# Meta keys of a head pair taken together in block 1's attention, and three convolution rows made ready one unit earlier

## The chip, the cores and the metric

The kernel runs on one core of a Trainium2 chip. The metric is the device time of one execution in microseconds (us). The names of the engines are those of the profile: PE multiplies matrices (PEld is its loading of weights), DVE works on vectors, ACT applies functions and copies, POOL is the general engine, SP issues the transfers.

## The reference, cut to what matters

The program is two transformer blocks on 256 tokens of width 1024. The change lies in the first one, whose mixer joins attention and a short convolution. The attention has 8 heads, each token sees 16 learned meta tokens and all tokens up to itself:

```python
N_META = 16; BLOCK = 128; N_HEADS = 8; QK_NOPE, QK_ROPE, V_DIM = 64, 32, 64
# for a block of 128 queries that starts at s0, keys = meta tokens + tokens:
s = (jnp.einsum('bqhd,bkhd->bhqk', qn_b, k_nope)
     + jnp.einsum('bqhr,bkr->bhqk', qr_b, k_rope)) * ATTN_SCALE
mask = (k_idx[None, :] >= PAD_FRONT) & (k_idx[None, :] <= q_idx[:, None])
p = jax.nn.softmax(jnp.where(mask[None, None], s, NEG_INF), axis=-1)
attn_block = jnp.einsum('bhqk,bkhd->bqhd', p, v)

u = gate_c * x_in                                    # the convolution beside it
y = sum(conv_w[k] * u_pad[:, k:k + plen] for k in range(CONV_W))
conv = gate_b * y
merged = concat([rms_norm(attn, attn_out_norm), rms_norm(conv, conv_out_norm)])
return merged @ w_out
```

Behind it come a routed mixture of 32 experts with a shared one, and the second block (pooling, windowed attention, a gated feed-forward part). They are not touched.

## The kernel before

The kernel is written out engine by engine: each engine has its own list of instructions, in the order of the code, and waits on counters (`s["..."]`) that other engines raise. No scheduler moves anything. An engine that waits holds up all that stands behind it in its list.

Block 1's attention is a loop over 16 **units** `u`. A unit is one head and one tile of 128 queries: `head_and_tile(u)` gives head 2·(u//4) + u%2 and tile u%4//2, so four units are a pair of heads with both tiles. Tile 0 sees 144 keys (16 meta, 128 tokens), tile 1 sees 272. Per unit:

- PE: `scores(u + 2)`, a share of other work, at every fourth unit `values` of the pair before, then `turn_probs(u)`, which turns the probabilities so that keys lie on the partitions (2 turns of 128 x 128 for tile 0, 3 for tile 1, the last one nearly empty: 16 keys).
- DVE: masked maximum of unit u (L1244), reciprocal and scaling of unit u-1 (L1250, L1251), then `beside(u)`.
- ACT: exponential of unit u (L739), two copies of the turned probabilities of unit u-1 from PSUM to SBUF (L748 for the full tiles, L749 for the 16 rows left over), then `beside(u)`.

The share of other work on PE is first the convolution: `conv_part(6)` to `conv_part(11)` in units 0 to 5, each 24 multiplications (three products of high and low halves, eight times), then from unit 7 on (`FILL = 7`) the convolution's rows times their part of `w_out`: `conv_share(j, m)`, two of them per unit, each 3 multiplications of 512 columns. `conv_share` with row tile m waits for `convg_done` m+1, and for the split weights.

For that, `beside` on ACT and DVE carries the convolution along. For each of the four row tiles m: ACT copies a gate out of PSUM (`conv_gate`, L670, which also frees the PSUM bank into which a later `conv_part` writes); DVE multiplies and adds the taps (`conv_taps`, L1160 to L1169) and the second gate (`conv_gated`, L1173); ACT squares the row tile (`conv_square`, L674) and makes its scaled high half (L725, counter `mrg_high`); DVE makes the low half (L1229, counter `convg_done`). Between these, ACT and DVE split weights into high and low halves of 1024 columns (`split_high_half` L403, `split_low_half` L410).

Before the change ACT makes the four high halves in unit 7 and DVE the four low ones in unit 8; `conv_gate(3)` stands in unit 5 behind a weight split. On PE `conv_part(11)` of unit 5 waits for `gc_sb` 4, which is `conv_gate(3)`.

`values(m, i)` multiplies the turned probabilities of a pair by its values: 4 multiplications for tile 0, 6 for tile 1, each of 64 columns of values with 128 queries; the two heads stand in the two halves of the PE columns and run side by side. The last pair's call stands behind the last unit, ahead of `mix_share`, the attention's rows times their part of `w_out`.

All weights come in 1 MB pieces through one SP queue, in the order of use. A piece is issued when PE (`split_used`, `used`) or another counter says that its place is free. Around the change these are: two work pieces that wait for `conv_done` and `convg_done` (L581), two ring pieces that wait for `split_used` of unit 15 (L592), three pieces that wait for the last `o_ps` (L581).

## Time and profile before

| | us |
|---|---|
| median of 3 runs | 682.7 (682.45 to 682.95) |
| the profiled execution | 681.71 |
| its span in the profile | 679.9 |

| engine | busy us, share of the span |
|---|---|
| PE | 629.5 (93%) |
| DVE | 356.8 (52%) |
| ACT | 293.8 (43%) |
| POOL | 49.3 (7%) |

The profile is of one execution. Times in its rows count from the start of the span. A timeline row gives start, duration, engine, source line, what is written and read, and how often; in square brackets stands the idle time of the engine ahead of it and what ended that. A row with xN is N instructions in a run, its duration from the first start to the last end. An fp32 multiplication on PE shows as two records, a turn of 128 columns as one. PEclk is the granted TensorE clock: 1.00 is 2.4 GHz, 0.50 is 1.2 GHz.

### The profile page before, as it was taken

The numbers are of one execution on the slowest core, as the hardware profiler recorded it, in microseconds if no ns is written. First come the engines' busy times: TensorE is split into PE (matmuls) and PEld (weight loads), VectorE is DVE, ScalarE is ACT, GpSimd is POOL, SyncE is SP. The second block draws the span as 40 slices with busy tenths as digits, with TensorE's granted clock in tenths as the row PEclk, the third lists the DMA queues.
The fourth block names the chain that finished last, engine by engine and source line by source line (L and its number), as shares of the span: only waits on it lengthen the run. The fifth ranks groups of instructions, "written<-read, shape, count | busy, mean of one in ns | idle before, by whom it ended". The sixth has DMA issues, their size and how long they took to land.

```text
span 679.9 us, 10209 instructions
## 1 busy us (share of the span) xinstructions
PE 629.5 (93%) x4027; PEld 471.7 (69%) x4027; DVE 356.8 (52%) x689; ACT 293.8 (43%) x560; POOL 49.3 (7%) x74
## 2 busy tenths in 40 slices
PE   8999799999999766779899999999999999999996
PEld 5979677842543321334389999898788888888884
DVE  5687664831130120110088886757856666666665
ACT  6855562421111010100085765554655555555554
POOL 2100101100010000000048100000000000000001
PEclk9999999999999976979999999999999999999999
DMA  8966328989999999999997443355535555555101
GB/s 345 421 231 240 126 123 330 408 362 425 428 388 421 421 421 419 423 421 421 421 422 291 155 150 124 124 187 187 185 134 192 196 199 193 195 193 185 63 1 62
DMA packets 26286, 180.73 MB, mean 266 GB/s; under 512 B 3184, under 2 KB 3312, under 8 KB 5120
## 3 DMA queue, kind: packets, MB, share of 16 engines
q1 hardware_dynamic: 25200, 177.60, 66.1%
q10 hardware_dynamic: 1040, 2.50, 0.9%
q8 instruction: 32, 0.52, 0.3%
q14 instruction: 14, 0.11, 0.1%
HBM read 179.04 MB, written 1.05 MB: 265 GB/s over the span
## 4 chain that ended last, share of the span: by engine, by line
PE 69%; DMA 15%; DVE 8%; ACT 5%; issue 2%; POOLq 0%; SPq 0%; POOL 0%; ACTq 0%; DVEq 0%
PE ps L1614 66%; DMA ring<-stream_dram 15%; PE ps L1617 3%; DVE ring_r L410 2%; ACT single L403 1%; DVE work L1549 1%; ACT work L889 1%; DVE work L1552 1%; DVE h L1602 0%; DVE work L1605 0%; ACT turned L894 0%; ACT work_r L885 0%; DVE extra_r L509 0%; DVE work L1430 0%; ACT work L799 0%
## 5 line engine op out<-in xcount | busy, mean ns | idle before, releaser
L1614 PE MATMUL ps<-turned,single 128*128 128x256 f32 (+2 forms) x944 | 231.3, 326 | 2.6 <-ACT work L670 1.8
L1614 PE MATMUL ps<-turned,ring_r 128*128 128x256 f32 (+1 forms) x648 | 179.8, 281 | 0.0
L1614 PEld LDWEIGHTS ps<-turned,single 128*128 128x128 f32 x944 | 156.3, 189 | 19.5 <-ACT work L670 2.4
L410 DVE TENSOR_TENSOR ring_r<-ring,single 128x1024 fp32r<-128x1024 f32 (+1 forms) x132 | 160.3, 1237 | 13.6 <-ACT single L403 13.4
L403 ACT ACTIVATE single<-ring 128x1024 fp32r<-128x1024 f32 (+1 forms) x132 | 134.1, 1047 | 0.1
L1614 PEld LDWEIGHTS ps<-turned,ring_r 128*128 128x128 f32 x648 | 121.1, 188 | 0.4
L1614 PE MATMUL ps<-ring,work 128*32 128x512 f32 (+2 forms) x462 | 71.0, 621 | 16.6 <-DMA ring<-stream_dram 14.3
L1614 PE MATMUL ps<-single,turned 128*128 128x512 f32 (+3 forms) x208 | 60.2, 369 | 2.9 <-DVE turned L1229 2.2
L1614 PEld LDWEIGHTS ps<-single 128*128 128x128 f32 x257 | 38.3, 188 | 34.2 <-issue 20.8
L1614 PE MATMUL ps<-single 128*128 128x512 f32 (+1 forms) x257 | 55.2, 353 | 3.4 <-DVE single L1441 2.3
L1614 PE MATMUL ps<-single,work_r 128*128 128x512 f32 x176 | 56.2, 392 | 0.0
L1614 PEld LDWEIGHTS ps<-ring,work 128*32 128x32 f32 (+1 forms) x462 | 19.9, 120 | 49.8 <-issue 23.2
L1582 DVE TENSOR_TENSOR work<-work,ps 128x512 f32<-128x512 f32 x22 | 15.1, 688 | 60.0 <-ACT work L919 59.8
L919 ACT ACTIVATE work<-ps 128x512 f32<-128x512 f32 x22 | 13.2, 598 | 73.1 <-PE ps L1614 73.1
L1614 PEld LDWEIGHTS ps<-single,turned 128*128 128x128 f32 (+1 forms) x208 | 36.7, 183 | 10.5 <-issue 2.5
L806 ACT ACTIVATE work<-ps 128x256 f32<-128x256 f32 x8 | 3.1, 384 | 91.6 <-PE ps L1614 91.6
L1614 PE MATMUL ps<-work 128*64 128x128 f32 (+7 forms) x272 | 38.8, 373 | 2.6 <-DVE work L1087 1.8
L1430 DVE TENSOR_TENSOR work<-work,ps 128x256 f32<-128x256 f32 x8 | 3.4, 422 | 70.4 <-ACT work L806 70.4
L1441 DVE SCALAR_TENSOR_TENSOR single<-ps,work,single 128x512 fp32r<-128x512 f32 x16 | 12.0, 751 | 52.7 <-ACT single L812 52.7
L1614 PEld LDWEIGHTS ps<-single,work_r 128*128 128x128 f32 x176 | 33.0, 187 | 7.3
L1614 PE MATMUL ps<-ring,turned_w 128*32 128x512 f32 x208 | 30.1, 688 | 8.0 <-DMA ring<-stream_dram 5.8
L1614 PE MATMUL ps<-ring_r,turned 128*128 128x512 f32 (+3 forms) x104 | 36.9, 363 | 0.0
(260 smaller groups left out, 703.6 us busy)
## 6 DMA issues: line engine op xcount, KB each, us to landing
ring<-stream_dram SPq DMA_DIRECT2D x145, 1024.0 KB, 11.9
work<-stream_dram SPq DMA_DIRECT2D x12, 1024.0 KB, 12.3
turned_w<-stream_dram SPq DMA_DIRECT2D x4, 1024.0 KB, 14.0
extra<-stream_dram SPq DMA_DIRECT2D x2, 1024.0 KB, 11.6
ring<-stream_dram SPq DMA_DIRECT2D x2, 832.0 KB, 7.6
h<-x_dram SPq DMA_DIRECT2D x2, 512.0 KB, 4.6
gain<-gains_dram ACTq DMA_DIRECT2D x2, 512.0 KB, 10.4
yields<-stream_dram SPq DMA_DIRECT2D x1, 1024.0 KB, 12.3
```

Source lines behind the costliest of these rows:

```text
L403: act.activation(w_hi[k % HIGHS][:, a], ring[:, place, a], ACT.Copy).then_inc(s["whi_done"], 1)
L410: dve.tensor_tensor(ring_r[:, place, a], ring[:, place, a], w_hi[k % HIGHS][:, a].bitcast(F32), ALU.subtract).then_inc(s["wlo_done"], 1)
L806: act.activation(sg, ps[:, 4, 0:FF], ACT.Silu).then_inc(s["sg_done"], 1)
L889: act.activation(gate[:, m, :], gate[:, m, :], ACT.Sigmoid).then_inc(s["sig_done"], 1)
L919: act.activation(fpart[:, m % 2, :].rearrange("p (a b) -> p a b", b=TOK), ffn_banks(m)[:, :, TOK:2 * TOK], ACT.Copy).then_inc(s["fsg_done" ...
L1430: dve.tensor_tensor(htok, sg, ps[:, 4, FF:2 * FF], ALU.mult).then_inc(s["ht_done"], 1)
L1441: dve.scalar_tensor_tensor(yl[:, n * 512:(n + 1) * 512], ps[:, 6 + n, :], wsl[:, p:p + 1], yh[:, n * 512:(n + 1) * 512].bitcast(F32), ALU. ...
L1549: dve.tensor_tensor(gate[:, m, :], gate[:, m, :], ps[:, 2 + m % 4, :], ALU.mult).then_inc(s["br_sb"], 1)
L1552: dve.tensor_tensor(gate[:, m, 0:TOK], gate[:, m, 0:TOK], gate[:, m, TOK:2 * TOK], ALU.add).then_inc(s["mg_sum"], 1)
L1582: dve.tensor_tensor(halves(fsum[:, m % 2, :], TOK), halves(fpart[:, m % 2, :], TOK), ffn_banks(m)[:, :, 0:TOK], ALU.add).then_inc(s["fh_su ...
L1614: return pe.matmul(o, lhsT, rhs, start=start, stop=stop, **kw)
L1617: return pe.transpose(o, a, ident[0:rows, 0:rows])
```

## The change

Each unit's 16 meta probabilities are scaled into a tile of their own, `pm1_meta`, where the two heads of a pair lie 32 columns apart in 64 columns with zeros between. They are turned once for both heads, at the odd unit, and multiplied with `v1_meta`, whose rows for the other head are zero. The tokens' keys now fill whole tiles of 128, and a multiplication of `values` takes both query tiles at once. ACT's `conv_gate(3)` goes from unit 5 to unit 4, ahead of the weight split; three of the high halves go to unit 6, the fourth stays at unit 7, and a weight split goes from unit 6 to unit 7; DVE's low halves go to units 7 and 8, and its `conv_taps(3)` ahead of a weight split.

```diff
             for i in range(NT):
                 act.wait_ge(s["v_ps"], i + 1)
+                act.activation(v1[i], ps[:, 4 + i, :], ACT.Copy).then_inc(s["v_sb"], 1)
+            act.wait_ge(s["v_ps"], NT + 1)
+            for j in range(2):
+                last = act.activation(v1_meta[j * META * 2:j * META * 2 + META, :].rearrange("p (a b) -> p a b", b=2 * VD)[:, :, j * VD:(j + 1) * VD],
+                                      ps[0:META, 6, :].rearrange("p (a b) -> p a b", b=2 * VD)[:, :, j * VD:(j + 1) * VD], ACT.Copy)
...
+                if u == 4:
+                    conv_gate(3)
                 if 2 <= u < 6:
                     split_high_half(act, 8 + (u - 2) // 2, u % 2)
                 if u == 5:
-                    conv_gate(3)
                     conv_square(2)
                 if u == 6:
+                    act.wait_ge(s["conv_ps"], 3 * CT)
+                    for m in range(CT - 1):
+                        conv_high(m)
+                if u == 7:
+                    conv_square(3)
+                    conv_high(CT - 1)
                     split_high_half(act, 10, 0)
-                if u == 7:
-                    act.wait_ge(s["conv_ps"], 3 * CT)
-                    conv_square(3)
-                    for m in range(CT):
-                        act.activation(mrg_hi[:, CT + m, :], mrg[:, m, :], ACT.Copy, ...
...
-                    act.activation(pt1[i][:, w % 2, 0:full_k], ps[:, 3 + w % 2, 0:full_k], ACT.Copy)
-                    act.activation(pt1[i][0:META, w % 2, full_k:full_k + P], ps[0:META, 3 + w % 2, full_k:full_k + P],
-                                   ACT.Copy).then_inc(s["pt_sb"], 1)
+                    i, j = w % 4 // 2, w % 2
+                    last = act.activation(pt1[:, j, i * P:(2 * i + 1) * P], ps[:, 3 + j, 0:(1 + i) * P], ACT.Copy)
+                    if j:
+                        last = act.activation(pt1_meta[0:4 * META, i * P:(i + 1) * P], ps[0:4 * META, 3 + j, TOK:TOK + P], ACT.Copy)
+                    last.then_inc(s["pt_sb"], 1)
...
                 if u == 6:
+                    conv_taps(3)
                     split_low_half(dve, 9, 1)
-                    conv_taps(3)
                 if u == 7:
                     conv_gated(3)
+                    conv_low(0)
+                    conv_low(1)
                 if u == 8:
-                    for m in range(CT): ...
+                    conv_low(2)
+                    conv_low(3)
...
-                    dve.tensor_scalar(pm1[:, w % 3, 0:nk], pm1[:, w % 3, 0:nk], rinv[:, w:w + 1], None, ALU.mult
+                    dve.tensor_scalar(pm1_meta[:, w % 4 // 2, w % 2 * 2 * META:w % 2 * 2 * META + META], pm1[:, w % 3, 0:META],
+                                      rinv[:, w:w + 1], None, ALU.mult)
+                    dve.tensor_scalar(pm1[:, w % 3, META:nk], pm1[:, w % 3, META:nk], rinv[:, w:w + 1], None, ALU.mult
...
-                for k in range(2 + head_and_tile(u)[1]):
-                    last = turn(ps[:, 3 + u % 2, k * P:(k + 1) * P], pm1[:, u % 3, k * P:(k + 1) * P])
+                i, j = u % 4 // 2, u % 2
+                for k in range(1 + i):
+                    last = turn(ps[:, 3 + j, k * P:(k + 1) * P], pm1[:, u % 3, META + k * P:META + (k + 1) * P])
...
+                if j:
+                    last = turn(ps[0:4 * META, 3 + j, TOK:TOK + P], pm1_meta[:, i, :])
...
-                u = 4 * m + 2 * i
-                pe.wait_ge(s["pt_sb"], u + 2)
+                pe.wait_ge(s["pt_sb"], 4 * (m + 1))
...
-                for k in range(2 + i):
+                for n, (v, a, lo) in enumerate(((v1[0], 0, 0), (v1[1], 2 * P, P), (v1_meta, None, 0))):
                     for j in range(2):
                         c = (2 * m + j) * VD
-                        last = mm(ps[j * VD:(j + 1) * VD, 6 + m % 2, i * P:(i + 1) * P], v1[k][:, c:c + VD],
-                                  pt1[i][:, j, k * P:(k + 1) * P], i == k == 0, i == 1 and k == 1 + i, skip_group_check=True)
+                        last = mm(ps[j * VD:(j + 1) * VD, 6 + m % 2, lo:TOK], v[:, c:c + VD],
+                                  pt1_meta if a is None else pt1[:, j, a:a + TOK - lo], n == 0, n == 2, skip_group_check=True)
```

Three places in the lists of instructions show what moved. First ACT, from unit 4 to unit 7, before the change. L403 is a weight split, L670 `conv_gate`, L674 `conv_square`, L725 the high halves, L748 and L749 the copies of turned probabilities.

```order
L749 ACTIVATE work<-ps 16x128
L403 ACTIVATE single<-ring 128x1024 [waits slot_full3,split_used]
L739 ACTIVATE work,stat<-work,stat 128x144 [waits nm_done]
L748 ACTIVATE work<-ps 128x128 [waits pt_ps]
L749 ACTIVATE work<-ps 16x128
L403 ACTIVATE single<-ring 128x1024
L670 ACTIVATE work<-ps 128x258 [waits cu_done,conv_ps]
L674 ACTIVATE work<-work 128x256 [waits conv_done]
L739 ACTIVATE work,stat<-work,stat 128x272 [waits nm_done]
L748 ACTIVATE work<-ps 128x128 [waits pt_ps]
L749 ACTIVATE work<-ps 16x128
L403 ACTIVATE single<-ring 128x1024 [waits slot_full4,split_used]
```

The same place on ACT with the change; L671 is `conv_gate` there, L404 a weight split, L675 `conv_square`, L678 a high half, L758 and L760 the copies.

```order
L760 ACTIVATE work<-ps 64x128
L671 ACTIVATE work<-ps 128x258 [waits cu_done,conv_ps]
L404 ACTIVATE single<-ring 128x1024 [waits slot_full3,split_used]
L750 ACTIVATE work,stat<-work,stat 128x144 [waits nm_done]
L758 ACTIVATE work<-ps 128x128 [waits pt_ps]
L404 ACTIVATE single<-ring 128x1024
L675 ACTIVATE work<-work 128x256 [waits conv_done]
L750 ACTIVATE work,stat<-work,stat 128x272 [waits nm_done]
L758 ACTIVATE work<-ps 128x128 [waits pt_ps]
L760 ACTIVATE work<-ps 64x128
L678 ACTIVATE turned<-work,vec 128x256 [waits conv_ps]
L678 ACTIVATE turned<-work,vec 128x256 x2
```

The gate copy has passed two weight splits and an exponential, the weight split of unit 6 has made way for three high halves, and the even unit has one copy of probabilities instead of two.

Second DVE, units 6 and 7, before the change: L1251 is the scaling of probabilities, L410 a weight split, L1160 to L1169 `conv_taps(3)`, L1244 the masked maximum (with a second instruction that reads it out).

```order
L1251 TENSOR_SCALAR work<-work,stat 128x144 [waits dve_step]
L410 TENSOR_TENSOR ring_r<-ring,single 128x1024 [waits whi_done]
L1160 TENSOR_TENSOR work<-work,ps 128x258 [waits conv_ps,gc_sb]
L1165 TENSOR_TENSOR work<-work 128x258 [waits z_sb,cu_done]
L1167 TENSOR_SCALAR work<-work,vec 128x256 [waits dve_step]
L1168 SCALAR_TENSOR_TENSOR work<-work,vec 128x256 [waits dve_step]
L1169 SCALAR_TENSOR_TENSOR work<-work,vec 128x256 [waits dve_step]
L1244 ISA work,stat<-ps,cst 128x272 [waits s_ps,dve_step]
```

The same place with the change; L1260 and L1262 are the two scalings, L411 the weight split.

```order
L1260 TENSOR_SCALAR work<-work,stat 128x16 [waits dve_step]
L1262 TENSOR_SCALAR work<-work,stat 128x128
L1165 TENSOR_TENSOR work<-work,ps 128x258 [waits conv_ps,gc_sb]
L1170 TENSOR_TENSOR work<-work 128x258 [waits z_sb,cu_done]
L1172 TENSOR_SCALAR work<-work,vec 128x256 [waits dve_step]
L1173 SCALAR_TENSOR_TENSOR work<-work,vec 128x256 [waits dve_step]
L1174 SCALAR_TENSOR_TENSOR work<-work,vec 128x256 [waits dve_step]
L411 TENSOR_TENSOR ring_r<-ring,single 128x1024 [waits whi_done,dve_step]
L1253 ISA work,stat<-ps,cst 128x272 [waits s_ps]
```

The taps stand ahead of the split, and each unit has one scaling more, of 16 columns.

Third PE, the last unit and the last `values`, before the change: L1617 is a turn, the rows with `ps<-work 64x128` are `values`, the last row is the first of `mix_share`.

```order
L1617 MATMUL ps<-cst,work 128x128 [waits pt_sb,p_done]
L1617 MATMUL ps<-cst,work 128x128 x2
L1614 MATMUL ps<-work 64x128 [waits att_low,pt_sb]
L1614 MATMUL ps<-work 64x128 x3
L1614 MATMUL ps<-work 64x128 [waits pt_sb]
L1614 MATMUL ps<-work 64x128 x5
L1614 MATMUL ps<-single,turned 128x512 [waits att_low,wlo_done,cm_sb]
```

The same place with the change.

```order
L1628 MATMUL ps<-cst,work 128x128 [waits pt_sb,p_done]
L1628 MATMUL ps<-cst,work 128x128
L1628 MATMUL ps<-cst,work 64x128
L1625 MATMUL ps<-work 64x256 [waits att_low,pt_sb]
L1625 MATMUL ps<-work 64x256
L1625 MATMUL ps<-work 64x128 x2
L1625 MATMUL ps<-work 64x256 x2
L1625 MATMUL ps<-single,turned 128x512 [waits att_low,wlo_done,cm_sb]
```

Two waits for copied probabilities, with four multiplications between them, have become one wait ahead of all six; the third turn writes 64 rows instead of 128.

## Rows read from the trace of the kernel before

**Rows 1.** The chain that ended last, in order: start us, us, what.

```profile
75.83 0.27 ACT work L670
...
82.58 0.67 DVE turned L1229
83.38 2.77 PE ps L1614 x6
...
205.46 13.52 DMA ring<-stream_dram
```

**Rows 2.** Stretches: us; busy of PE, PEld, DVE, ACT, POOL; PEclk; DMA share; GB/s.

```profile
90.00:100.00 10.00, 9.87 (x66) 7.78 (x65) 7.98 (x21) 6.96 (x22) 0.74 (x1) 1.00 0.01 2
...
190.00:200.00 10.00, 9.48 (x77) 4.07 (x79) 4.87 (x13) 2.14 (x4) 2.39 (x3) 1.00 0.96 378
...
210.00:220.00 10.00, 9.38 (x47) 3.21 (x45) 0.75 (x1) 1.07 (x2) 0.00 (x0) 1.00 1.01 424
```

**Rows 3.** Timeline of SP: the first transfers behind the last units.

```profile
104.14 0.80 SPq L592 DMA_DIRECT2D ring<-stream_dram  x2
106.58 1.30 SPq L581 DMA_DIRECT2D work<-stream_dram  x3
```

**Rows 4.** Timeline of units 5 and 6, PE and ACT.

```profile
75.73 0.36 ACT L670 ACTIVATE work<-ps 128x258 f32<-128x258 f32 x1
...
76.15 0.51 PE L1614 MATMUL ps<-turned,single 128*128 128x256 f32 x2 [1.26 <-ACT work L670]
...
79.13 0.38 PE L1617 MATMUL ps<-cst,work 128*128 128x128 f32 x2
79.34 0.41 PE L1614 MATMUL ps<-work 128*128 128x144 f32 x2
...
79.87 1.04 ACT L403 ACTIVATE single<-ring 128x1024 fp32r<-128x1024 f32 x1
...
80.41 0.55 PE L1617 MATMUL ps<-cst,work 128*128 128x128 f32 x3 [0.66 <-DVE work L1251]
```

**Rows 5.** Timeline of unit 7: the high and low halves, and PE behind them.

```profile
82.05 1.69 ACT L725 ACTIVATE turned<-work,vec 128x256 fp32r<-128x256 f32 x4
...
82.58 1.84 DVE L1229 SCALAR_TENSOR_TENSOR turned<-work,vec,turned 128x256 fp32r<-128x256 f32 x4 [0.56 <-ACT turned L725]
83.38 0.64 PE L1614 MATMUL ps<-single,turned 128*128 128x512 f32 x1 [2.17 <-DVE turned L1229]
...
86.58 0.80 PE L1614 MATMUL ps<-work 128*128 128x272 f32 x2
```

**Rows 6.** Stretches of 1 us in both waits; columns as in rows 2.

```profile
75.00:76.00 1.00, 0.00 (x0) 0.00 (x0) 0.14 (x1) 1.00 (x2) 0.00 (x0) 1.00 0.00 0
...
84.00:85.00 1.00, 1.00 (x4) 0.81 (x3) 0.96 (x6) 0.14 (x2) 0.00 (x0) 0.50 1.02 426
```

**Rows 7.** Timeline of PE: a weight load behind `values`, and unit 8.

```profile
73.98 0.20 PEld L1617 LDWEIGHTS ps<-cst,work 128*128 128x128 f32 x2 [0.17 <-issue]
...
88.14 0.40 PE L1614 MATMUL ps<-ring_r,turned 128*128 128x512 f32 x1
88.38 0.40 PE L1614 MATMUL ps<-single,turned 128*128 128x512 f32 x1
88.70 1.31 PE L1614 MATMUL ps<-work 128*64 128x128 f32 x20
```

**Rows 8.** Timeline of the attention's end, PE and ACT.

```profile
104.50 0.55 PE L1617 MATMUL ps<-cst,work 128*128 128x128 f32 x3 [0.17 <-DVE work L1251]
104.98 1.56 PE L1614 MATMUL ps<-work 128*64 128x128 f32 x20
...
105.37 0.25 ACT L749 ACTIVATE work<-ps 16x128 f32<-16x128 f32 x1
106.47 0.50 PE L1614 MATMUL ps<-single,turned 128*128 128x512 f32 x1
```

**Rows 9.** Groups of DVE by form: busy us, mean ns, idle before.

```profile
L1436 DVE TENSOR_SCALAR work<-work 128x16 f32<-128x16 f32 x1 | 0.2, 175 | 0.0
```

More of the change, by code:

```diff
@@ L674, in conv_square, with conv_high @@
                 act.activation(sq[:, CT + m, :], mrg[:, m, :], ACT.Square).then_inc(s["sq_done"], 1)
+            def conv_high(m):
+                act.activation(mrg_hi[:, CT + m, :], mrg[:, m, :], ACT.Copy,
+                               scale=vec[:, V_GCONV + m:V_GCONV + m + 1]).then_inc(s["mrg_high"], 1)
             split_high(act, 4)
@@ L697, in _ @@
             act.wait_ge(s["pad_done"], 1)
-            for i, m in enumerate((P, P, META)):
+            for i in range(NT):
                 act.wait_ge(s["v_ps"], i + 1)
-                act.activation(v1[i][0:m, :], ps[0:m, 4 + i, :], ACT.Copy).then_inc(s["v_sb"], 1)
+                act.activation(v1[i], ps[:, 4 + i, :], ACT.Copy).then_inc(s["v_sb"], 1)
[3 more added lines that the diff above has]
+                                      ps[0:META, 6, :].rearrange("p (a b) -> p a b", b=2 * VD)[:, :, j * VD:(j + 1) * VD], ACT.Copy)
+            last.then_inc(s["v_sb"], 1)
             for hp in range(0, HEADS // 2, 2):
@@ L1174, in conv_gated, with conv_low @@
                                   ).then_inc(s["conv_done"], 1)
+            def conv_low(m):
+                dve.wait_ge(s["mrg_high"], m + 1)
+                dve.scalar_tensor_tensor(mrg_lo[:, CT + m, :], mrg[:, m, :], vec[:, V_GCONV + m:V_GCONV + m + 1],
+                                         mrg_hi[:, CT + m, :].bitcast(F32), ALU.mult, ALU.subtract).then_inc(s["convg_done"], 1)
             conv_taps(0)
@@ L1840, in _ @@
                 if u and u % 4 == 0:
-                    values(u // 4 - 1, 0)
-                    values(u // 4 - 1, 1)
+                    values(u // 4 - 1)
                 turn_probs(u)
@@ L1857, in mix_share @@
                         last.then_inc(s["mix_ps"], 1)
-            values(CT - 1, 0)
-            values(CT - 1, 1)
+            values(CT - 1)
             pe.wait_ge(s["cm_sb"], 2 * NT)
```

46 lines of the change are left out of this document (16 added, 30 removed).

## The prediction

> **What bounds the kernel now.** I read the chain of waits first, then the stretches, then the timeline of the stage that changes. In the chain the reader is to see three things [rows 1]: it passes through ACT's gate copy (L670) at 75.83 us and through the low halves of the convolution (L1229) at 82.58 us, runs on PE behind them, and from 205.46 us on it waits for weight transfers. So a gain in the attention must also reach the transfers to count. The stretches answer that [rows 2]: from 90 to 100 us the queue moves 2 GB/s, it is empty, since places for weights are not free yet; its next pieces are issued at 104.14 and 106.58 us, released by PE in the last unit and by the last `values` [rows 3]. From 210 on it moves 424 GB/s at a share of 1.01. Between, at 190 to 200 us, its share is still 0.96: it waits for PE there. The stream therefore begins when the attention ends and its last gap is closed by PE. If the attention ends X earlier, both PE and the stream move by X, and the end too.
>
> In the timeline of the attention PE is busy except for two places. In unit 5 it stands 1.26 us for the gate copy, which ACT makes at 75.73 only because a weight split is ahead of it [rows 4]. In units 6 and 7 it waits 0.66 us for the scaling of unit 6 [rows 4] and 2.17 us for the first low half [rows 5]. Behind this second wait the granted clock is 0.50, which is 1.2 GHz; in the first wait, and behind it, it stayed at 1.00 [rows 6].
>
> **The change part by part.** Gains have a plus.
>
> *Gate copy in unit 4.* `conv_gate(3)` needs `conv_part(9)`, done a unit before, so it no longer ends last. What is late next for `conv_part(11)` is PE itself. +1.26 [rows 4].
>
> *High and low halves in units 6 to 8.* Before, the first `conv_share` begins at 83.38, that is 1.33 after ACT begins the high halves at 82.05 [rows 5]. With the change the high halves stand where the weight split stood that began at 79.87 [rows 4], right behind the copy of unit 5. On the old times the first share begins at 79.87 + 1.33 = 81.20, which is 2.18 earlier. PE would be ready at about 80.2 (scores at 79.34, three turns and one more scores behind), so some 1.0 us of waiting is left. The wait of 0.66 for the scaling is inside these 2.18: the taps pass the weight split on DVE and the gate comes earlier, so the maxima of units 7 and 8 no longer queue behind both. +2.18. Bounds: the rest of the wait goes wholly (+3.2), or one more weight split of 1.04 stays ahead (+1.1).
>
> *The clock.* From 83.38 to 86.58, 3.20 us, PE runs at 0.50 [rows 5, 6]. If the remaining wait of 1.0 does not lower the clock, and the 1.26 did not, the same work takes half of it. +1.6. Bounds: 0 and +1.6.
>
> *Turns.* A pair has 2 + 2 + 3 + 3 turns before and 1 + 2 + 2 + 3 now, 8 fewer in four pairs. Two turns take from 79.13 to 79.34, 0.11 each [rows 4]. +0.9; where PE waits beside one it is worth nothing, so 0 to +0.9.
>
> *Columns of PE changed over.* The eight turns of meta keys have 64 columns, between turns and scores of 128. The rows show what such a change costs at `values`: the last two multiplications of a share stand 0.24 apart, the first of `values` 0.32 behind the last (88.14, 88.38, 88.70), 0.08 more, and behind `values` no weights are loaded for 0.17 us [rows 7]. Each of the eight goes in and out, but the last one is followed by `values`, in the same mode: 15 changes. I take 0.10, nearer to the difference of starts, since an idle weight load is partly covered: -1.5, with 1.2 and 2.6 as ends. The Trainium skill (TensorEngine Tiling (Array Packing), Key Properties) says that changing the tiling mode drains the engine; the trace agrees with its 0.08, the page has no price.
>
> *`values`.* 10 multiplications of 128 queries become 4 of 256 and 2 of 128: the same 640 columns streamed for each head, so no gain. But the last one now waits for the whole copy. Before, its first four multiplications ran from 104.98 beside the copies, the rest followed at the copy's end, 105.37 + 0.25 = 105.62, and `mix_share` began at 106.47 [rows 8]. Now all 1.31 us [rows 7] stand behind 105.62, which gives 106.93: -0.5. For the first three pairs a share or a `conv_part` lies between copy and `values` and hides it.
>
> *DVE and ACT.* Each unit has one scaling of 16 columns more; the only such row takes 0.175 us [rows 9]. It counts where PE waits for the scaling, as at 104.50 [rows 8]; about one unit in each pair after the first, so -0.2, with 0 and 16 x 0.175 = -2.8 as ends. ACT drops one of two copies (0.25 us) in the eight even units; PE covers that, so 0. The longer clearing on POOL and the two copies of meta values lie before the loop, beside `conv_part(4)` and `(5)`: 0; uncovered, the second copy would cost about the 0.25 of such a copy.
>
> *Transfers.* The two work pieces that wait for `conv_done` and `convg_done` are issued some 2 to 4 us earlier, into an empty queue. 0.
>
> Sum: 1.26 + 2.18 + 1.6 + 0.9 - 1.5 - 0.5 - 0.2 = 3.7 us. Against the profiled execution, 681.71, that is 678.0. This execution was 1.0 below the median of 682.7, so for the median I predict 682.7 - 3.7 = 679.0.
>
> **The rivals.** Two runs of this kernel apart by less than 0.2%, 1.4 us, are not told apart.
>
> *The narrow turn takes two passes.* A turn shows as one record, an ordinary fp32 multiplication as two: `values` has 20 records for 10 [rows 7]. If the 64-column turn is run like an ordinary one, each of the eight costs 0.11 more, 0.9 in all: 679.9. Against it: no turn of 64 columns is in the trace; that the turned data pass through exactly needs no second pass. The Trainium skill (same page, Gotcha 2) says that column tiling excludes the transpose mode for fp32 input; by that rule this case would be the likely one, and no row here can show it.
>
> *The wait for the low halves stays long.* If ACT reaches the high halves late (its instruction waits for the end of all convolution parts, behind the copy of unit 5) the wait is again near 2 us, and the clock falls again: 1.6 and about 1.1 of the 2.18 are lost, 682.7 - 1.0 = 681.7. For it: the clock did fall behind 0.66 + 2.17. Against it: the copy ahead of it is released by a turn that PE makes right after the last part.
>
> *The stream takes it.* If transfers and not PE set the time of the stage behind, nothing is left: 682.7. For it: the chain is on transfers from 205 us [rows 1]. Against it: the queue moves 2 GB/s at 90 to 100 us and is restarted by PE [rows 2, 3].
>
> *Slower.* The mode changes drain more than `values` shows, because a turn is only 0.11 long and the scores and shares behind it queue up. Without their price the sum is 5.2; the 15 changes decide from 0.35 us each (5.2 / 15), and at 0.44 the kernel is slower by 1.4: 684.1. Against it: 0.08 to 0.17 at `values` [rows 7].
>
> *Changes for nothing.* If a turn of 64 columns is loaded like any other, the 1.5 fall away: 677.5.
>
> **How the numbers follow.** Forecast 0.60, two passes 0.12, wait stays 0.08, stream 0.06, slower 0.05, changes for nothing 0.09. Forecast's own range: 1.1 less by the mode changes' upper end and 0.9 less by turns beside waits give 681.0; 0.3 more by their lower end, and the rest of the wait gone (1.0), 677.7. The range for all reaches a little past the free changes and to the long wait: 677.2 to 681.6. Faster: 0.60 + 0.12 + 0.09 = 0.81; within the bound: 0.14; slower: 0.05.
>
> **What would show it.** Right: no PE wait for the gate copy in unit 5; the first share of 512 columns about 3.4 us (1.26 + 2.18) earlier; no stretch at 0.50 between 75 and 100 us; a step of about 0.1 us on either side of each 64-column turn; a wait of some 0.6 us ahead of the last `values`; the transfer of 106.58 at about 102.9, and the first transfer wait of 205.46 about 3.7 earlier. Wrong: two records for a turn of meta keys; a clock of 0.50 behind the first share; the first transfers earlier but the wait at 205 unmoved; or a new wait for scalings in most units.

## The result and the profile after

| | before | after |
|---|---|---|
| median of 8 runs | 682.95 (682.1 to 684.41) | 678.44 (676.41 to 679.84) |
| ratio of the times, 95% interval | | 0.9928 (0.9914 to 0.9941) |
| profiled execution, its span | 681.71, 679.9 | 676.90, 675.1 |

The change makes the kernel 0.7% faster, 4.9 us by the ratio. The forecast was 679.0 with a range of 677.2 to 681.6. Profiled execution against profiled execution the sum of the forecast's terms was 3.7 us and the measured difference is 4.8: the direction and the main mechanism were right, and one term stood for a cost that is not there.

The timeline of PE of the changed kernel, from the first `values` to the first row of `mix_share`, answers to the PE rows of [rows 4, 5, 7, 8]. L1625 is a multiplication, L1628 a turn.

```profile
72.73 1.30 PE L1625 MATMUL ps<-work 128*64 128x256 f32 x12
...
74.39 0.60 PE L1625 MATMUL ps<-turned,single 128*128 128x256 f32 x2
...
77.44 0.38 PE L1628 MATMUL ps<-cst,work 128*128 128x128 f32 x2
77.66 0.41 PE L1625 MATMUL ps<-work 128*128 128x144 f32 x2
...
79.35 0.47 PE L1625 MATMUL ps<-single,turned 128*128 128x512 f32 x1 [0.75 <-DVE turned L1183]
...
81.41 0.59 PE L1625 MATMUL ps<-single,turned 128*128 128x512 f32 x1
...
90.62 0.55 PE L1628 MATMUL ps<-cst,work 128*128 128x128 f32 x3 [0.39 <-DVE work L1262]
...
98.96 0.55 PE L1628 MATMUL ps<-cst,work 128*128 128x128 f32 x3 [0.41 <-DVE work L1262]
100.14 1.30 PE L1625 MATMUL ps<-work 128*64 128x256 f32 x12 [0.63 <-ACT work L760]
101.37 0.50 PE L1625 MATMUL ps<-single,turned 128*128 128x512 f32 x1
```

Two rows of the kernel before belong beside them, its first `values` and unit 8's share:

```profile
72.74 1.31 PE L1614 MATMUL ps<-work 128*64 128x128 f32 x20
...
87.01 0.60 PE L1614 MATMUL ps<-single,turned 128*128 128x512 f32 x1
```

The row at 74.39 is `conv_part(11)`: no wait in brackets is left, where it stood at 76.15 with 1.26. The first share stands at 79.35 instead of 83.38, 4.03 earlier; its wait is 0.75 instead of 2.17 us. From it to unit 8's share (81.41, before 87.01) it is 2.06 instead of 3.63 us. The last row, `mix_share`, is 5.10 earlier than at 106.47 [rows 8]. Three rows show what the change gives back: the waits for scalings at 90.62 and 98.96, and 0.63 us ahead of the last `values`, which stood without a wait before.

The halves and the clock: ACT makes the high halves (L678) and DVE the low ones (L1183) in the changed kernel:

```profile
78.19 1.29 ACT L678 ACTIVATE turned<-work,vec 128x256 fp32r<-128x256 f32 x3
...
78.72 0.88 DVE L1183 SCALAR_TENSOR_TENSOR turned<-work,vec,turned 128x256 fp32r<-128x256 f32 x2 [0.53 <-ACT turned L678]
```

Stretches of the changed kernel, in the columns of [rows 2]:

```profile
79.00:80.00 1.00, 0.65 (x3) 0.60 (x4) 0.82 (x4) 1.00 (x5) 0.00 (x0) 1.00 0.80 164
90.00:100.00 10.00, 8.71 (x50) 6.26 (x49) 6.63 (x24) 6.47 (x22) 0.73 (x1) 1.00 0.09 16
100.00:110.00 10.00, 9.86 (x53) 7.88 (x54) 2.73 (x7) 0.83 (x3) 1.01 (x1) 1.00 0.99 417
190.00:200.00 10.00, 10.00 (x84) 3.85 (x76) 2.52 (x4) 1.37 (x2) 2.39 (x3) 1.00 0.94 362
...
210.00:220.00 10.00, 8.38 (x56) 4.06 (x55) 1.68 (x3) 1.76 (x3) 0.00 (x0) 1.00 1.01 423
```

The granted clock is 1.00 behind the wait of 0.75, so the stretch at 0.50 of [rows 6] is gone. The share of the transfers still has a gap at 190 to 200 and is full at 210, as in [rows 2]. SP's issues and the first long transfer in the chain:

```profile
98.36 0.80 SPq L593 DMA_DIRECT2D ring<-stream_dram  x2
101.48 1.29 SPq L582 DMA_DIRECT2D work<-stream_dram  x3
```

```profile
195.23 8.31 DMA ring<-stream_dram
```

The issue of 106.58 [rows 3] stands at 101.48, 5.10 earlier, as much as `mix_share`; 4.8 of it reach the end of the span. The wait of 195.23 has no counterpart in the chain of before. The next long one has; first before, then after, it starts 5.04 and ends 4.25 earlier:

```profile
220.70 18.16 DMA ring<-stream_dram
```

```profile
215.66 18.95 DMA ring<-stream_dram
```

### The profile page after: what moved, and what is told of

Its sections match the earlier page's. It is cut to its first block, busy times and chain, and to the rows that moved or that the text cites. A ratio compares the mean times of both kernels' runs of the same rounds, so it can differ in the third digit from the quotient of the medians.

```text
span 675.1 us, 10135 instructions
## 1 busy us (share of the span) xinstructions
PE 628.7 (93%) x3987; PEld 470.5 (70%) x3987; DVE 359.2 (53%) x705; ACT 292.9 (43%) x553; POOL 49.4 (7%) x72
## 3 DMA queue, kind: packets, MB, share of 16 engines
HBM read 179.04 MB, written 1.05 MB: 267 GB/s over the span
## 4 chain that ended last, share of the span: by engine, by line
PE 71%; DMA 14%; DVE 8%; ACT 4%; issue 2%; POOLq 0%; SPq 0%; POOL 0%; ACTq 0%; DVEq 0%
PE ps L1625 68%; DMA ring<-stream_dram 14%; PE ps L1628 3%; DVE ring_r L411 2%; ACT single L404 1%; DVE work L1560 1%; ACT work L900 1%; DVE work L1563 1%; DVE h L1613 0%; DVE work L1616 0%; ACT turned L905 0%; ACT work_r L896 0%; DVE extra_r L510 0%; DVE work L1441 0%; ACT work L810 0%
## 5 line engine op out<-in xcount | busy, mean ns | idle before, releaser
L1625 PE MATMUL ps<-turned,single 128*128 128x256 f32 (+2 forms) x944 | 231.5, 327 | 1.3 <-DVE turned L1578 0.6
L1625 PE MATMUL ps<-turned,ring_r 128*128 128x256 f32 (+1 forms) x648 | 179.7, 281 | 0.0
L1625 PEld LDWEIGHTS ps<-turned,single 128*128 128x128 f32 x944 | 156.4, 189 | 18.0 <-issue 2.0
L411 DVE TENSOR_TENSOR ring_r<-ring,single 128x1024 fp32r<-128x1024 f32 (+1 forms) x132 | 159.8, 1233 | 11.2 <-ACT single L404 11.0
L404 ACT ACTIVATE single<-ring 128x1024 fp32r<-128x1024 f32 (+1 forms) x132 | 134.1, 1047 | 0.1
L1625 PEld LDWEIGHTS ps<-turned,ring_r 128*128 128x128 f32 x648 | 121.1, 188 | 0.4
L1625 PE MATMUL ps<-ring,work 128*32 128x512 f32 (+2 forms) x462 | 71.0, 621 | 18.1 <-DMA ring<-stream_dram 15.8
L1625 PEld LDWEIGHTS ps<-single 128*128 128x128 f32 x257 | 38.3, 189 | 33.9 <-issue 20.5
L1625 PE MATMUL ps<-single,turned 128*128 128x512 f32 (+3 forms) x208 | 59.2, 364 | 1.6 <-DVE ring_r L411 0.9
L1625 PE MATMUL ps<-single 128*128 128x512 f32 (+1 forms) x257 | 55.3, 353 | 3.5 <-DVE single L1452 2.3
L1625 PE MATMUL ps<-single,work_r 128*128 128x512 f32 x176 | 56.2, 392 | 0.0
L1625 PEld LDWEIGHTS ps<-ring,work 128*32 128x32 f32 (+1 forms) x462 | 19.9, 120 | 50.4 <-issue 24.8
L1625 PEld LDWEIGHTS ps<-single,turned 128*128 128x128 f32 (+1 forms) x208 | 36.2, 181 | 9.0 <-DVE ring_r L411 1.6
L1625 PE MATMUL ps<-work 128*64 128x128 f32 (+7 forms) x240 | 38.5, 400 | 3.2 <-DVE work L1092 1.8
L1625 PEld LDWEIGHTS ps<-single,work_r 128*128 128x128 f32 x176 | 33.0, 187 | 7.3
L1028 POOL TENSOR_SCALAR stat<-stat 128x1 f32<-128x1 f32 (+1 forms) x7 | 4.7, 666 | 437.5 <-ACT ps L945 177.7
L1625 PE MATMUL ps<-ring_r,turned 128*128 128x512 f32 (+3 forms) x104 | 36.4, 358 | 0.0
```

The costliest lines, as they stand in the source:

```text
L404: act.activation(w_hi[k % HIGHS][:, a], ring[:, place, a], ACT.Copy).then_inc(s["whi_done"], 1)
L411: dve.tensor_tensor(ring_r[:, place, a], ring[:, place, a], w_hi[k % HIGHS][:, a].bitcast(F32), ALU.subtract).then_inc(s["wlo_done"], 1)
L1028: pool.tensor_scalar(ms, ss, 1.0 / D, EPS, ALU.mult, ALU.add).then_inc(s["pool_step"], 1)
L1625: return pe.matmul(o, lhsT, rhs, start=start, stop=stop, **kw)
```

## The experiments

All kernels are compared inside one stage, since executions of one kernel differ by 2 to 3.5 us (682.10 to 684.41 before, 676.41 to 679.84 after), as much as many of the effects. The **count** is the time from the start of the first `values` to the start of the first row of `mix_share`. "To share" is from the first `values` to the first share of 512 columns, "to unit 8" from there to unit 8's share. Us, from the timelines of PE, one profiled execution per kernel; the ratio is that of the times to the kernel before, with its interval. The first `values` start between 72.58 and 74.68 us in these executions, so points in time that the expectations name, such as `mix_share` at 101.1, shift by up to 2 us; the differences do not.

| kernel | to share | to unit 8 | count | ratio |
|---|---|---|---|---|
| before | 10.64 | 3.63 | 33.73 | |
| after | 6.62 | 2.06 | 28.64 | 0.9928 (0.9914 to 0.9941) |
| e1_rows | 6.75 | 2.07 | 28.28 | 0.9923 (0.9904 to 0.9943) |
| e2_meta | 10.20 | 3.60 | 33.74 | 0.9988 (0.9976 to 1.0000) |
| e3_gate | 10.33 | 3.64 | 33.45 | 1.0001 (0.9990 to 1.0013) |
| e4_warm | 10.64 | 2.05 | 32.17 | 0.9963 (0.9949 to 0.9977) |
| e8_taps | 9.11 | 3.86 | 33.37 | 0.9972 (0.9955 to 0.9989) |
| e9_high | 8.49 | 2.05 | 30.01 | 0.9943 (0.9921 to 0.9966) |
| e5_wide | 6.63 | 2.06 | 28.61 | 0.9925 (0.9904 to 0.9947) |
| e6_tail | 6.62 | 2.46 | 28.68 | 0.9915 (0.9893 to 0.9937) |
| e7_early | 6.08 | 2.77 | 28.47 | 0.9922 (0.9900 to 0.9945) |
| e10_order | 6.08 | 2.78 | 28.18 | 0.9932 (0.9910 to 0.9955) |
| e11_rows_early | 6.23 | 2.24 | 27.94 | 0.9939 (0.9918 to 0.9959) |
| e12_low | 6.08 | 2.36 | 27.88 | 0.9925 (0.9908 to 0.9941) |

The first question is which half of the change gains, the rows or the meta keys. **The rows alone** (e1_rows):

```diff
+                if u == 4:
+                    conv_gate(3)
                 if 2 <= u < 6:
...
                 if u == 5:
-                    conv_gate(3)
...
                 if u == 6:
+                    act.wait_ge(s["conv_ps"], 3 * CT)
+                    for m in range(CT - 1):
+                        conv_high(m)
+                if u == 7:
+                    conv_square(3)
+                    conv_high(CT - 1)
                     split_high_half(act, 10, 0)
...
                 if u == 6:
+                    conv_taps(3)
                     split_low_half(dve, 9, 1)
-                    conv_taps(3)
                 if u == 7:
                     conv_gated(3)
+                    conv_low(0)
+                    conv_low(1)
...
```

> The kernel before with the changed order of the convolution rows alone (gate copy in unit 4, three high halves in unit 6, the fourth in unit 7, low halves in units 7 and 8, taps ahead of the split); the meta keys are turned and multiplied as before. Theory (the rows are the gain, the meta keys nearly nothing): conv_part(11) at 74.4 to 74.6 instead of 76.15, the first share of 512 columns at 79.5 to 80.1 instead of 83.38, granted clock 1.00 throughout 75 to 100 us, mix_share at 101.1 to 101.7 instead of 106.47, the time 4.8 to 5.4 us under the kernel before. The forecast's own terms give 1.26 + 2.18 + 1.6 = 5.0 here as well. Rival (much of the gain came from the meta keys, that is from fewer turns and multiplications): gain of 3 us or less, mix_share at 103 or later.

```profile
73.33 1.31 PE L1623 MATMUL ps<-work 128*64 128x128 f32 x20
...
80.08 0.47 PE L1623 MATMUL ps<-single,turned 128*128 128x512 f32 x1 [0.66 <-DVE turned L1183]
...
101.61 0.50 PE L1623 MATMUL ps<-single,turned 128*128 128x512 f32 x1
```

The count is 28.28, a gain of 5.45, and the clock stays at 1.00: the whole gain and 0.36 more than the full change has in this count. **The meta keys alone** (e2_meta) is the changed kernel with these places put back:

```diff
-                if u == 4:
-                    conv_gate(3)
...
-                    conv_low(0)
-                    conv_low(1)
...
```

> The changed kernel with the order of the convolution rows put back as before; the meta keys of a pair are still turned and multiplied together. Theory (a turn of 64 columns between turns of 128 is free; eight turns fewer give 0.9 at most, the scalings of 16 columns and the last values take 0.5 to 1.0): both waits of 1.3 and 2.2 us and the stretch at clock 0.50 are back, mix_share between 106.2 and 106.8 (before: 106.47), the time within 0.5 us of the kernel before. The forecast's terms (0.9 - 1.5 - 0.5 - 0.2): 1.3 us slower, mix_share at 107.8.

```profile
76.45 0.51 PE L1621 MATMUL ps<-turned,single 128*128 128x256 f32 x2 [1.13 <-ACT work L671]
...
83.50 0.77 PE L1621 MATMUL ps<-single,turned 128*128 128x512 f32 x1 [1.98 <-DVE turned L1181]
```

The waits are back, and the stretch at 0.50 with them. The count is that of before, 33.74 for 33.73. Only ahead of it does the meta part show a gain: from the first turn to the first `values` 14.69 us (58.61 to 73.30) instead of 14.90 (57.84 to 72.74). So the forecast's 1.3 us of loss for the meta part is not there. The time's ratio leaves anything from no change to 1.6 us.

Of this, **the price of the column change** was tried by itself (e5_wide), a meta turn of full width in the changed kernel:

```diff
-                    last = turn(ps[0:4 * META, 3 + j, TOK:TOK + P], pm1_meta[:, i, :])
+                    last = turn(ps[:, 3 + j, TOK:TOK + P], pm1_meta[:, i, :])
```

> The changed kernel with the meta turn 128 columns wide instead of 64 (the 64 further columns hold zeros and their result is not read), so that no change of column width stands between turns and scores. Theory (a change of width costs nothing here): step of 0.11 us for this turn as for the others, from the first values to mix_share 28.5 to 28.8 us as in the changed kernel (28.64), time within 0.2 us of it. The forecast's term (15 changes of 0.10): 1.4 us less for the whole attention, 27.6 in this count (three quarters of the turns lie in it). Rival by 0.17 a change: 2.5 us less.

The count is 28.61 for 28.64. PE's timeline has the same two turns of unit 5 here, both 128 wide:

```profile
79.19 0.38 PE L1628 MATMUL ps<-cst,work 128*128 128x128 f32 x2
79.41 0.41 PE L1625 MATMUL ps<-work 128*128 128x144 f32 x2
```

They take 0.22 us up to the scores. In the changed kernel, where the second of them has 64 columns, it is 0.22 as well (77.44 to 77.66), and in the kernel before 0.21 [rows 4]. The groups by form of the changed kernel show the narrow turns with no time idle ahead of them (the last column):

```profile
L1628 PE MATMUL ps<-cst,work 128*64 128x128 f32 x8 | 2.2, 272 | 0.0
```

A change of width costs nothing here, and eight records for eight turns refute the rival of two passes. The Trainium skill (TensorEngine Tiling (Array Packing), Key Properties) has a change of the tiling mode drain the engine; this trace shows no such time at a turn of 64 columns.

Next the parts of the rows. **The gate copy alone** (e3_gate):

```diff
+                if u == 4:
+                    conv_gate(3)
                 if u == 5:
-                    conv_gate(3)
```

> The kernel before with one edit: the gate copy conv_gate(3) in unit 4 instead of unit 5. Theory: conv_part(11) at 74.4 to 74.6 instead of 76.15, that is 1.6 to 1.8 earlier; ACT still makes the high halves behind the weight split of unit 6, so the first share of 512 columns moves less than that, to between 82.0 and 83.0, the wait ahead of it grows to 2.5 to 3.5 us, and the granted clock falls to 0.50 behind it as before; gain in time 0.4 to 1.4 us. Rival (the two waits are one chain, and the gate alone takes both away): first share before 81.5, clock 1.00, gain 3 us or more.

The wait of 1.26 is gone, the count is only 0.28 lower, and the time has not changed. PE's timeline in units 6 and 7 shows where it went:

```profile
80.26 0.55 PE L1618 MATMUL ps<-cst,work 128*128 128x128 f32 x3 [2.20 <-DVE work L1252]
82.91 0.54 PE L1615 MATMUL ps<-single,turned 128*128 128x512 f32 x1 [1.86 <-DVE turned L1230]
```

Before, the waits were 1.26 + 0.66 + 2.17 = 4.09 us; now they are 2.20 + 1.86 = 4.06. The expectation that the last of them grows was wrong, and with it the gain of 0.4 to 1.4 us: the time went to the wait before it. DVE's timeline names the holder:

```profile
75.71 1.23 DVE L410 TENSOR_TENSOR ring_r<-ring,single 128x1024 fp32r<-128x1024 f32 x1 [2.59 <-ACT single L403]
...
76.85 0.42 DVE L1161 TENSOR_TENSOR work<-work,ps 128x258 f32<-128x258 f32 x1
...
79.28 0.44 DVE L1245 CUSTOM_DVE_ANT_0 work<-ps,cst 128x272 f32<-128x272 f32 x1
```

DVE waits 2.59 us for ACT's weight split, makes its own, and only then the taps (from 76.85) and the maximum that the scaling needs. **Gate and taps** (e8_taps) take that away:

```diff
+                if u == 4:
+                    conv_gate(3)
...
                 if u == 5:
-                    conv_gate(3)
...
                 if u == 6:
+                    conv_taps(3)
                     split_low_half(dve, 9, 1)
-                    conv_taps(3)
```

> The gate copy in unit 4 (which alone moved the wait of 1.26 us to the scaling of unit 6, 2.20 us) together with conv_taps(3) ahead of the weight split on DVE in unit 6; the high and low halves stay in units 7 and 8. Counted from the start of the first values to the start of mix_share (before 33.73, gate alone 33.45, all row edits 28.28). Theory (the taps behind the split held the scaling, so gate and taps are one step): no wait for the scaling of unit 6 above 0.3 us; the high halves still stand behind a weight split and unit 7's work on ACT, so the first share comes 1.0 to 1.9 us earlier than before in this count and waits 2 to 3 us, the clock falls to 0.50 behind it; 31.9 to 32.8, gain in time 0.9 to 1.8 us. Rival (gate and taps do nothing without the high halves): 33.2 to 33.7. Rival (they do it all): 28.3 to 29.5, clock 1.00.

The wait for the scaling is gone and the first share comes 1.53 us earlier in this count, as the theory had it; but the count gains 0.36 in all, as the first rival had it. PE's timeline, and stretches in the columns of [rows 2], the last one from the kernel before:

```profile
82.50 0.77 PE L1615 MATMUL ps<-single,turned 128*128 128x512 f32 x1 [3.00 <-DVE turned L1230]
```

```profile
82.00:83.00 1.00, 0.50 (x1) 0.50 (x2) 1.00 (x3) 1.00 (x4) 0.07 (x1) 0.50 1.03 434
...
87.00:88.00 1.00, 1.00 (x3) 0.74 (x3) 0.74 (x2) 1.00 (x2) 0.00 (x0) 0.50 0.99 393
88.00:89.00 1.00, 1.00 (x6) 0.54 (x4) 0.46 (x4) 0.57 (x3) 0.00 (x0) 0.81 0.30 123
```

```profile
86.00:87.00 1.00, 1.00 (x6) 0.93 (x5) 0.00 (x0) 0.17 (x1) 0.00 (x0) 0.54 1.08 459
```

All the waiting stands in one place now, 3.00 us, and the clock is at 0.50 until past 88, where before it rose at 86.9. Of the 1.53 us that the first share gained, 0.23 are lost up to unit 8's share and 0.94 behind it (20.40 us from there to `mix_share`, before 19.46), at the slower clock; 0.36 are left. The timed runs gain more (0.8 to 3.1 us) than this one execution; whether the clock falls for as long in each of them is open.

**The halves alone** (e9_high): the high and low halves as changed, gate and taps as before.

```diff
                 if u == 6:
+                    act.wait_ge(s["conv_ps"], 3 * CT)
+                    for m in range(CT - 1):
+                        conv_high(m)
+                if u == 7:
+                    conv_square(3)
+                    conv_high(CT - 1)
                     split_high_half(act, 10, 0)
...
                 if u == 7:
                     conv_gated(3)
+                    conv_low(0)
+                    conv_low(1)
...
```

> The high halves in units 6 and 7 and the low halves in units 7 and 8 as in the change, the weight split behind them, but the gate copy stays in unit 5 and the taps stay behind the split. Theory (the forecast's 2.18 without its 0.66, since the waits in units 5 and 6 stay): the first share 1.4 to 2.2 us earlier than before, a wait of 0.3 to 1.2 us ahead of it, so the clock stays 1.00 there; from the first values to mix_share 29.9 to 31.0 us (before 33.73), gain in time 2.7 to 3.8 us. Rival (the two waits of units 5 and 6 together lower the clock too): a stretch at 0.50, 31.5 or more.

```profile
77.25 0.51 PE L1622 MATMUL ps<-turned,single 128*128 128x256 f32 x2 [1.26 <-ACT work L670]
...
81.51 0.55 PE L1625 MATMUL ps<-cst,work 128*128 128x128 f32 x3 [0.68 <-DVE work L1259]
82.33 0.47 PE L1622 MATMUL ps<-single,turned 128*128 128x512 f32 x1
```

PE's timeline has both earlier waits, 1.26 and 0.68, and the third is gone, where 0.3 to 1.2 us of it were expected; the clock stays at 1.00. The count is 3.72 lower: 2.15 at the first share and 1.58 behind it. Gate and taps give 1.73 on top of it (30.01 to 28.28), and 0.36 without it.

**The clock alone** (e4_warm): nine multiplications that nobody reads are put into the wait ahead of the first share.

```diff
+                if f == 0:
+                    split_ready(9, 0)
+                    idle_products(ps[:, 7, :], w_hi[0][:, 0:P], w_hi[0][:, 0:512], 9)
```

> The kernel before with nine multiplications of 512 columns whose result nobody reads, put into the wait ahead of the first share of 512 columns (into a PSUM bank that is free there); everything else as before. Theory (the clock fell because PE stood idle for 2.17 us and cost about 1.6 us by itself): the first share stays at 83.4 (82.8 to 83.9), the granted clock stays 1.00 behind it, unit 8's share is reached 2.0 to 2.1 instead of 3.63 us after the first, mix_share at 104.9 to 105.4, gain 1.1 to 1.6 us. Rival (the clock falls anyway at this place, or the slow stretch comes from something else than idleness): 3.6 us between the two shares, no gain.

```profile
82.88 2.34 PE L1614 MATMUL ps<-single 128*128 128x512 f32 x9
85.32 0.47 PE L1614 MATMUL ps<-single,turned 128*128 128x512 f32 x1
```

```profile
85.00:86.00 1.00, 0.90 (x4) 0.63 (x4) 1.00 (x4) 1.00 (x4) 0.00 (x0) 1.00 1.09 459
```

The first share comes no earlier (10.64 in both), but the clock is 1.00 behind it, and unit 8's share follows 2.05 instead of 3.63 us later. The count gains 1.56: with the wait unchanged, this is the price of the clock by itself (the times give 1.6 to 3.5 us).

Last, what the changed kernel still leaves. **The last `values` cut up** (e6_tail), tile 0's queries ahead of the last wait:

```diff
+                split = m == CT - 1
+                pe.wait_ge(s["pt_sb"], 4 * (m + 1) - (2 if split else 0))
...
+                if split:
+                    some[0:1] = [(v1[0], 0, 0, P), (v1[0], P, P, TOK)]
```

> The changed kernel with the last values cut up so that the two multiplications of tile 0's queries run before the copies of the last units are waited for, as the kernel before had it; the first two multiplications of the last pair are four of 128 queries. Theory: from the last turn of unit 15 to mix_share 1.95 to 2.1 us as before (1.97) instead of 2.41, so 28.2 to 28.3 from the first values to mix_share; a wait of 0.3 us or less between the two parts. Rival (the copy's end sets it anyhow): 2.35 to 2.45.

From the last turn to `mix_share` it takes 2.19 us (99.67 to 101.86), between the two expectations: the changed kernel takes 2.41 (98.96 to 101.37), the one before 1.97. The wait between the two parts is 0.26, as expected. The count, 28.68, misses its range and does not fall, since unit 8's share came 0.40 later behind a long low half on DVE (1.03 us), which the next kernels show too; the edit does not touch that place. **The first high half earlier** (e7_early, with the cut `values`) puts it on ACT ahead of the copy of unit 5:

```diff
+                    if u == 6:
+                        act.wait_ge(s["conv_ps"], 3 * CT)
+                        conv_high(0)
                     act.wait_ge(s["pt_ps"], w + 1)
```

> The changed kernel with the last values cut up (two multiplications of tile 0's queries ahead of the last wait) and with the first high half ahead of the copy of unit 5 on ACT in unit 6, so that it waits for the last convolution part only and not for the turn and copies behind it. Theory (ACT's two copies, 0.33 us, and the turn before them are all that keeps PE waiting 0.75 us): the first share 0.4 to 0.6 us earlier, the wait ahead of it 0.15 to 0.35 us; from the first values to mix_share 27.7 to 28.1 us (changed kernel 28.64), 0.5 to 0.9 us faster than it. Rival (the copies, pushed back by the high half, hold the next turns, or DVE's low half comes no earlier): 28.3 or more.

The first share comes 0.54 earlier with a wait of 0.20, as expected, but unit 8's share again later, so the count, 28.47, misses its range and stands where the rival had it. **The scaling of 16 columns behind that of the tokens** (e10_order, on top of it):

```diff
+                    dve.tensor_scalar(pm1[:, w % 3, META:nk], ...).then_inc(s["p_done"], 1)
+                    dve.tensor_scalar(pm1_meta[...], ...).then_inc(s["pmeta_done"], 1)
```

> As the kernel with the cut values and the early high half, and further with DVE's scaling of 16 meta columns behind the scaling of the tokens, with a counter of its own that only the meta turn waits for. Theory (the two waits of 0.39 and 0.41 us for scalings were 0.17 to 0.2 before because the 16 columns stood ahead): each falls to about 0.2 to 0.3, since the first turn no longer waits for 0.14 us; 0.2 to 0.3 us less than without this edit, 27.4 to 27.9 from the first values to mix_share. Rival (the meta turn stands a step behind the tokens' and waits for as much): no difference above 0.1 us.

The waits of 0.39 and 0.43 fall to 0.24 and 0.29, the count by 0.29, as expected, though to 28.18 and not below 27.9, since unit 8's share is still late. The late share of unit 8 shows in the timelines of DVE and POOL of this kernel:

```profile
80.71 1.03 DVE L1185 SCALAR_TENSOR_TENSOR turned<-work,vec,turned 128x256 fp32r<-128x256 f32 x1
```

```profile
80.73 0.73 POOL L1004 TENSOR_TENSOR work<-work 128x256 f32<-128x256 f32 x1 [2.92 <-ACT work L675]
```

The third low half takes 1.03 us where others take 0.48; it begins 0.02 us ahead of POOL's addition, and unit 8's share waits for it. **The third low half in unit 7** (e12_low, on top of that) takes it out of this place:

```diff
                     conv_low(1)
+                    conv_low(2)
                 if u == 8:
-                    conv_low(2)
                     conv_low(3)
```

> As the kernel with ordered scalings, and further with the third low half on DVE in unit 7 instead of unit 8, so that it no longer starts together with POOL's addition of squares (80.71 and 80.73 us, where it took 1.03 us for 0.48 and held unit 8's share by some 0.5 us). Theory: unit 8's share 2.0 to 2.4 us after the first share instead of 2.78, no instruction of the low halves longer than 0.7 us unless it meets POOL again; the maximum of unit 8 and the scaling of unit 7 come 0.2 us later; 27.6 to 28.0 from the first values to mix_share (28.18 without the edit). Rival (the low half delays the scaling by as much as it gives): 28.1 to 28.4.

Unit 8's share follows 2.36 us after the first instead of 2.78, and the count is 27.88, both as expected; the longest low half, 0.71 us, is again beside POOL. And **the rows with the early high half, without the meta part** (e11_rows_early), the edits of e1_rows and the early high half on the kernel before:

> The kernel before with the changed order of the convolution rows and the early high half; the meta keys as before (so neither its scaling nor its turns). Theory (the meta part is worth nothing, the rows all): the first share 0.4 to 0.5 us earlier than with the rows alone (6.75 from the first values), from the first values to mix_share 27.7 to 28.0 us (rows alone 28.28), time 5.3 to 6.0 us under the kernel before. Rival (the meta part gains once the waits are gone): this kernel 0.3 us or more behind the one with meta part, cut values and ordered scalings.

The count is 27.94, within 0.1 us of all edits with the meta part together (27.88); the 0.2 us that the meta part gains ahead of the first `values` are not in the count. The last three have counts 0.5 to 0.8 us under the changed kernel's, but ratios of 0.9925 to 0.9939 for its 0.9928, and intervals that overlap: no version is shown to beat it.

## Why the prediction was right, and where it was not

- **Gate copy, +1.26.** In the full change `conv_part(11)` starts 1.76 earlier: a turn less makes 0.11, the rest is a wait longer than the trace listed. The listed idle time counts from the end of the scores' record, 74.26 + 0.62 = 74.88; without a wait `conv_part(11)` starts 0.26 behind the scores' start (74.13 to 74.39 after), so that the wait of before was worth 1.89 - 0.26 = 1.63. But the term does not stand by itself: without the taps and the halves it is worth 0.28 (e3_gate), with the taps 0.36 (e8_taps), and with the halves the two give 1.73. The prediction summed it as if each wait were its own, which held only since all were moved together.
- **Halves, +2.18.** Right in the full change, for which it was worked out: 4.03 - 1.76 = 2.27, with a wait of 0.75 left where 1.0 was named; that it would not lower the clock held. The 2.15 of the halves alone (e9_high) are near it by chance: there no wait is left ahead of the share, and the 0.68 ahead of the turns stays.
- **The clock, +1.6.** Right: 3.63 - 2.06 = 1.57, and 1.56 with nothing else changed (e4_warm).
- **Turns +0.9, `values` -0.5, scalings -0.2.** From unit 8's share to `mix_share` before takes 106.47 - 87.01 = 19.46 us and after 101.37 - 81.41 = 19.96, so 0.5 is lost. The end behind the last turn costs 2.41 - 1.97 = 0.44, as forecast, and its new wait of 0.63 is the one that was named. The scalings cost 0.24 at the last turn (a wait of 0.41 for 0.17) and 0.26 at 90.62, where the turns start 0.78 us behind the last multiplication of the share and at the same place of before 0.52 (95.65 to 96.17): 0.5 against the 0.2 of the forecast. The four turns saved in this stretch give 0.42 back.
- **No gain inside `values`.** Right: 640 columns for each head take 1.24 us up to the next turn, before (72.74 to 73.98) and after (72.73 to 73.97). The description of the kernel has the two heads run side by side. The trace shows no time gained by it: 20 records of 128 columns in 1.24 us are 0.48 ns for a column, and a share's 512 columns in 0.24 us (88.14 to 88.38) are 0.47.
- **The sum.** At `mix_share` the terms measured in the two executions are 1.76 + 2.27 + 1.57 - 0.5 = 5.1, the difference there.
- **Columns changed over, -1.5: the step that failed.** The prediction took 0.08 to 0.17 us from `values` and priced 15 changes at 0.10. The runs show none (e5_wide, 28.61 for 28.64). What stood beside `values` was no price of the width of a turn; what it is was not tried. Without the term the sum is the rival's, 5.2, for which 677.5 was named; 4.8 was measured in the profiled executions and 4.5 between the medians. That the median of 678.44 lies in the forecast's own range (677.7 to 681.0) is in part luck: its lower end counted on the rest of the wait going (1.0), and that wait stayed; the gain came out larger because the changes cost nothing. That rival had a chance of 0.09, too little: the only evidence against it came from multiplications of another kind.
- **The rivals.** Two passes: ruled out by the eight records. The wait stays long: it fell to 0.75. The stream takes it: 5.1 us at `mix_share` became 4.8 at the end, though the mark was wrong: the first long transfer wait comes 10.2 us earlier (195.23 for 205.46), not 3.7, since it is a wait that the chain of before does not have; the one behind it starts 5.04 and ends 4.25 earlier. The slower case rested on the mode changes and fell with them.

The gain is therefore that of the convolution's rows: 5.45 in the count without the meta part. The meta part alone gains 0.2 ahead of the first `values` and nothing behind, and on top of the rows it gives some 0.4 back (28.28 to 28.64) through `values` and scalings.

## What to carry to other kernels

Waits on one engine that stand in a row behind the same two helpers can act as one wait: here taking away the first moved its time to the next, and only an edit that reached the last of them shortened the stage by much (3.72 us in the count against 0.28 and 0.36). Count the clock with the last wait, since a shorter way to a longer wait can lose in clock what it gains. And a price read from one kind of instruction is a bound for another kind, not its value: a gap beside a multiplication said nothing of a turn.

## What the runs showed of the hardware

- PE's idle time and its clock: 0.75 us (after) and 1.26 and 0.68 us in a row (e9_high) left the granted clock at 1.00. 2.17 us behind 0.66 (before) were followed by 0.50 for some 3.4 us, and 3.00 us (e8_taps) for some 7. Multiplications that nobody reads, kept up through the wait, kept it at 1.00 (e4_warm). The length of one wait does not decide it: in e3_gate the clock was still at 1.00 behind a wait of 2.20 us, and fell to 0.50 behind the next one, of 1.86. Two stretches of that kernel:

```profile
80.00:81.00 1.00, 0.74 (x5) 0.58 (x5) 0.96 (x6) 0.54 (x3) 0.00 (x0) 1.00 0.00 0
...
84.00:85.00 1.00, 1.00 (x4) 0.72 (x4) 0.55 (x4) 0.00 (x0) 0.00 (x0) 0.50 1.05 426
```

- DVE and POOL hinder each other. A low half that meets an addition of squares on POOL takes some 0.7 to 1.03 us instead of 0.48, and ends 0.28 to 0.29 us behind the addition: in e10_order 81.74 for 81.46, in e6_tail 82.12 for 81.83, in e9_high 84.61 for 84.32, in e12_low 82.05 for 81.77. In the changed kernel both are long:

```profile
80.63 1.35 DVE L1183 SCALAR_TENSOR_TENSOR turned<-work,vec,turned 128x256 fp32r<-128x256 f32 x2
80.64 1.05 POOL L1002 TENSOR_TENSOR work<-work 128x256 f32<-128x256 f32 x1 [3.14 <-ACT work L675]
```

There the third low half takes 0.48, POOL 1.05 and the fourth low half 0.96 (to 81.98, POOL to 81.69), and unit 8's share is not held. In e6_tail the same two start as close together (81.08 and 81.09), and it is the third low half that is long, so what their starts by the profile decide is open. The Trainium skill (SBUF — State Buffer, SBUF: two separate sides) states that the port pair of these two engines, for a DVE instruction with two SBUF inputs beside a POOL instruction that reads SBUF, is held by one of them for its whole instruction, by whichever starts first; the long records fit the first half of that, and their starts lie too close to tell the second.
